# Five top-k steps moved to earlier slots, sparse scores in groups, and the first slabs' cuts on one engine, in a hybrid decoder block on one core

## The reference

```python
h = rmsnorm(x, norm_mix)
q_sb,k_sb,v_sb, q_sa,k_sa,v_sa, q_idx,k_idx,w_idx, g_sb,g_sa = split(h @ w_in)
# branch A, 8 heads: stick-breaking attention
z = q_sb @ k_sb.T / 8                               # q, k normed per head
attn = exp(log_sigmoid(z) + sum over later keys j<t of log_sigmoid(-z))   # strictly causal
o_sb = attn @ v_sb
# branch B, 8 heads, 2 key heads: sparse attention
score = sum over 8 index heads of w_idx * relu(q_idx @ k_idx.T / sqrt(32)) # causal
idx = top_k(score, 128)                             # per query
s = q_sa @ k_sa[idx].T / 8 - slope * distance ;  o_sa = softmax(s) @ v_sa[idx]
x = x + (sigmoid(g_sb) * (o_sb @ w_branch_sb) + sigmoid(g_sa) * (o_sa @ w_branch_sa)) @ w_out
x = x + relu(rmsnorm(x, norm_mlp) @ w_ff1)**2 @ w_ff2
```

## Time and profile before

| | |
|---|---|
| median of 3 runs | 729.56 us (729.49 to 729.64) |
| profiled execution | 729.32 us, its span 727.6 us |
| TensorE busy | 721.1 us (99% of the span) |
| VectorE, ScalarE, GpSimd busy | 523.4, 336.1, 242.7 us |
| HBM | 93 GB/s over the span |

### The profile page before, as it was taken

The page is one execution under the profiler, slowest core; times in us unless marked ns, Lnnn a source line. Parts: engine busy times, 40 slices in busy tenths (PEclk is TensorE's granted clock), DMA queues, the critical chain, the costliest instruction groups (busy, mean ns, idle before and its releaser), DMA issues.

```text
span 727.6 us, 9748 instructions
## 1 busy us (share of the span) xinstructions
PE 721.1 (99%) x3456; PEld 575.6 (79%) x3456; DVE 523.4 (72%) x757; ACT 336.1 (46%) x483; POOL 242.7 (33%) x197
## 2 busy tenths in 40 slices
PE   8999999999999999999999999999999999999998
PEld 5878788787776666788889988888888888888887
DVE  7355887899986865537746569695968778695972
ACT  6244753465567777722334353534344252535320
POOL 4005226011224663003301091815336180816610
DMA  9309231311111202133190225151331505131102
GB/s 327 145 15 264 84 117 58 116 59 59 59 59 36 78 11 52 59 116 115 45 331 5 78 92 175 59 173 58 118 112 54 177 0 182 49 115 58 58 16 101
DMA packets 44037, 70.62 MB, mean 97 GB/s; under 512 B 2657, under 2 KB 27489, under 8 KB 44002
## 3 DMA queue, kind: packets, MB, share of 16 engines
q1 hardware_dynamic: 44000, 70.16, 29.6%
q10 hardware_dynamic: 2, 0.00, 0.0%
HBM read 65.71 MB, written 2.10 MB: 93 GB/s over the span
## 4 chain that ended last, share of the span: by engine, by line
PE 92%; DVE 4%; ACT 1%; POOL 1%; issue 1%; DMA 0%; DVEq 0%; ACTq 0%; POOLq 0%
PE ps L1849 8%; PE ps L1848 8%; PE ps L1847 8%; PE ps L422 6%; PE ps L424 6%; PE ps L423 6%; PE ps L1875 6%; PE ps L1877 6%; PE ps L1876 6%; PE ps L415 6%; PE ps L417 5%; PE ps L416 5%; PE ps L1729 1%; PE ps L1665 1%; PE ps L1699 1%; PE ps L1761 1%
## 5 line engine op out<-in xcount | busy, mean ns | idle before, releaser
L1847 PE MATMUL ps<-b_hi,cut_hi 128*128 128x512 f32 (+1 forms) x280 | 104.0, 371 | 0.0
L1848 PE MATMUL ps<-b_lo,cut_hi 128*128 128x512 f32 (+1 forms) x280 | 103.8, 371 | 0.0
L1849 PE MATMUL ps<-b_hi,cut_lo 128*128 128x512 f32 (+1 forms) x280 | 103.8, 371 | 0.0
L422 PE MATMUL ps<-cut_hi,a_hi 128*128 128x512 f32 x216 | 86.5, 400 | 0.0
L424 PE MATMUL ps<-cut_hi,a_lo 128*128 128x512 f32 x216 | 84.5, 391 | 0.0
L423 PE MATMUL ps<-cut_lo,a_hi 128*128 128x512 f32 x216 | 84.3, 390 | 0.0
L917 ACT ACTIVATE qo_sb<-ps 128x512 f32<-128x512 f32 x32 | 19.1, 598 | 135.6 <-PE ps L1849 91.0
L636 POOL TENSOR_TENSOR a_lo<-qo_sb,a_hi 128x512 fp32r<-128x512 f32 x49 | 78.2, 1628 | 5.6 <-ACT a_hi L927 5.6
L406 DVE TENSOR_TENSOR cut_lo<-raw,cut_hi 128x2048 fp32r<-128x2048 f32 (+2 forms) x33 | 53.4, 1622 | 27.6 <-ACT cut_hi L398 27.6
L398 ACT ACTIVATE cut_hi<-raw 128x2048 fp32r<-128x2048 f32 (+2 forms) x33 | 48.5, 1468 | 31.1 <-PE ps L417 22.7
L1848 PEld LDWEIGHTS ps<-b_lo,cut_hi 128*128 128x128 f32 x280 | 52.8, 188 | 9.1
(11 more groups left out here) (210 smaller groups left out, 1678.3 us busy)
## 6 DMA issues: line engine op xcount, KB each, us to landing
raw<-in_w_ff_dram SPq DMA_DIRECT2D x32, 1024.0 KB, 5.6
raw<-in_w_in_dram SPq DMA_DIRECT2D x16, 1024.0 KB, 5.6
gates<-in_x_dram SPq DMA_DIRECT2D x8, 512.0 KB, 5.7
raw<-in_w_out_dram SPq DMA_DIRECT2D x4, 1024.0 KB, 5.1
raw<-in_w_in_dram SPq DMA_DIRECT2D x4, 512.0 KB, 7.1
raw<-in_w_branch_sb_dram SPq DMA_DIRECT2D x2, 1024.0 KB, 4.9
raw<-in_w_branch_sa_dram SPq DMA_DIRECT2D x4, 512.0 KB, 6.1
out_dram<-gates SPq DMA_DIRECT2D x7, 256.0 KB, 2.0
```

Of the source, the lines that this page charges most:

```text
L422: nc.tensor.matmul(dst, l_hi, w_hi, start=start, stop=False)
L1847: T.matmul(dst, w_hi[:, w], b_hi[:, k, a:b], start=(k == 0), stop=False)
L1848: T.matmul(dst, w_hi[:, w], b_lo[:, k, a:b], start=False, stop=False)
L1849: mm = T.matmul(dst, w_lo[:, w], b_hi[:, k, a:b], start=False, stop=(k == KD - 1))
```

## The change

Three edits.

1. The lower half of slab 1's low part goes from GpSimd (between its second and third row norm) to VectorE, between VectorE's two other cuts.
2. Top-k: two steps per token block in QSA where there was one, and five behind it where there were four; of the eight single steps in the sparse heads those at n = 8, 9 and 10 stay. The slots between keep their counts.
3. Scores: the pairs 0 to 3 (first token block) are computed together inside the last gate of the stick-breaking heads, pairs 4 and 5 together at pair 2 and pairs 6 and 7 together at pair 4; from pair 8 on it is one at a time as before. `score_bank` puts the pairs of a group side by side in the two banks that hold the scores, and `sa_logits` waits for the whole group. In the last stick-breaking pair the first head's sums come after one group of three gate matmuls in place of two.

```diff
--- before.py
+++ after.py
@@ -429,6 +429,12 @@
         def gate_bank(f):
             return 6 if f == 0 or f >= 8 and f % 2 else 7
 
+        def score_bank(n):
+
+            b, r = divmod(n // 2, GQ)
+            a = (r * P, r % 2 * 2 * P, 0, 0)[b]
+            return bank(n % 2, a, a + (b + 1) * P)
+
         def sa_head(n):
 
             r, g = divmod(n % 8, SAKV)
@@ -568,11 +574,6 @@
                                    ALU.pow).then_inc(row_ready, 1)
 
             for m in range(TB):
-                if m == 2:
-                    pool.wait_ge(half_hi, 2)
-                    pool.wait_ge(half_cut, 1)
-                    pool.tensor_tensor(cut_slot(1, cut_lo, 0, 2), raw[:, 1, 0:SLAB // 2],
-                                       cut_slot(1, cut_hi, 0, 2).bitcast(F32), ALU.subtract).then_inc(half_cut, 1)
                 rows_rsqrt(m)
 
             n_norm = 0
@@ -1070,6 +1071,7 @@
             norm_lo(1, a_hi, a_lo)
             norm_scale(1, x_tok[:, 1, :], x_tok[:, 1, :], mix_gain)
             dve_cut(0, 1, 2)
+            dve_half(1)
             dve_cut(1, 1, 2)
             for m in range(2, TB):
                 norm_lo(2 * m - 2, a_hi, a_lo)
@@ -1188,7 +1190,7 @@
                             V.tensor_copy(k_stack[:, :], k_in)
                             V.tensor_copy(q_stack[:, 4:8, :], q_in[:, 4:8, :]).then_inc(ix_ready, 1)
                         if g >= KSB:
-                            topk(1)
+                            topk(2 if g == QSA else 1)
                         head_scaled(4 * g + m)
                 else:
                     for m in range(TB):
@@ -1198,7 +1200,7 @@
                 if g in (KSB, QSA):
                     dve_cut(2 * g + 3)
                 if g in (KSB, QSA):
-                    topk(4)
+                    topk(5 if g == QSA else 4)
 
             def zset(h):
                 return ps[:, 3 * (h % 2) * S:3 * (h % 2) * S + ZW]
@@ -1229,12 +1231,12 @@
             def sa_logits(n):
 
                 w, j = (n // 8 + 1) * P, n % 4
-                dve.wait_ge(s_done, n + 1)
+                dve.wait_ge(s_done, 8 if n < 8 else n // 4 * 4 + 4 if n < 16 else n + 1)
                 dve.wait_ge(bias_done, n + 1)
                 dve.wait_ge(tri_done, 7 if n < 2 else 8)
                 if n >= 4:
                     dve.wait_ge(pt_done, n - 3)
-                V.tensor_tensor_reduce(out=sa_s[j][:, 0:w], in0=bank(n % 2, 0, w), in1=sa_bias[j][:, 0:w],
+                V.tensor_tensor_reduce(out=sa_s[j][:, 0:w], in0=score_bank(n), in1=sa_bias[j][:, 0:w],
                                        scale=-1.0, scalar=3.0e38, op0=ALU.add, op1=ALU.min,
                                        accum_out=snmax[:, j:j + 1]).then_inc(smax_done, 1)
 
@@ -1266,7 +1268,7 @@
                 V.tensor_scalar(sa_s[j][:, 0:w], sa_s[j][:, 0:w], rcp_l[:, j:j + 1], None, ALU.mult).then_inc(pn_done, 1)
                 if n < 32:
                     sa_logits(n)
-                topk(1 if n in (4, 7, 8, 9, 10, 11, 12, 15) else 0 if n < 20 else 60)
+                topk(1 if n in (8, 9, 10) else 0 if n < 20 else 60)
                 if n % 8 in (5, 6) and n < 32:
                     if n == 5:
                         dve.wait_ge(lo_done, SL_GATE + 5)
@@ -1720,14 +1722,15 @@
                 if k1 == KD:
                     mm.then_inc(gate_done, 1)
 
-            def sa_scores(pair):
-                b, r = divmod(pair, GQ)
-                if pair:
-                    pe.wait_ge(smax_done, 2 * pair)
-                for g in range(SAKV):
-                    p = slice(64 * g, 64 * g + 64)
-                    T.matmul(bank(g, 0, (b + 1) * P), qT_sa[p, r, b * P:(b + 1) * P],
-                             k_sa[p, 0:(b + 1) * P], start=True, stop=True).then_inc(s_done, 1)
+            def sa_scores(first, count=1):
+                if first:
+                    pe.wait_ge(smax_done, 2 * first)
+                for pair in range(first, first + count):
+                    b, r = divmod(pair, GQ)
+                    for g in range(SAKV):
+                        p = slice(64 * g, 64 * g + 64)
+                        T.matmul(score_bank(2 * pair + g), qT_sa[p, r, b * P:(b + 1) * P],
+                                 k_sa[p, 0:(b + 1) * P], start=True, stop=True).then_inc(s_done, 1)
 
             pe.wait_ge(const_cut, 2)
             pe.wait_ge(tr_out, 16)
@@ -1740,16 +1743,16 @@
                 gate(2 * c)
                 if c:
                     weighted_values(c - 1)
-                gate(2 * c + 1, 0, 2)
+                early = 1 if c == 3 else 2
+                gate(2 * c + 1, 0, early)
                 sum_later(2 * c)
-                gate(2 * c + 1, 2, 6)
+                gate(2 * c + 1, early, 6)
                 sum_later(2 * c + 1)
                 if c == 3:
                     pe.wait_ge(a_done, 7)
-                    sa_scores(0)
+                    sa_scores(0, 4)
                 gate(2 * c + 1, 6, 8)
             weighted_values(3)
-            sa_scores(1)
 
 
             def sa_turn(n):
@@ -1781,7 +1784,10 @@
                     gate(15, *((0, 2), (2, 3))[pair - 14])
                 sa_turn(2 * pair + 1)
                 if pair < 14:
-                    sa_scores(pair + 2)
+                    if pair in (2, 4):
+                        sa_scores(pair + 2, 2)
+                    elif pair >= 6:
+                        sa_scores(pair + 2)
                     gate(8 + pair // 2, 4 * (pair % 2) + 2, 4 * (pair % 2) + 4)
                 if pair and pair % 2 == 0:
                     sa_values(pair // 2 - 1)
```

## The result

| | before | after |
|---|---|---|
| median | 729.49 us (729.21 to 729.65, 20 runs) | 730.58 us (729.94 to 731.34, 20 runs) |
| profiled execution | 729.32, span 727.6 | 730.15, span 728.4 |
| ratio | | 1.0015 (95%: 1.0009 to 1.0021) |

The change costs 1.09 us, 0.15%: less than the 0.2% that was set as the limit of "same", and measurable all the same. The forecast was 730.2 and "same".

What follows compares the result with a forecast made beforehand. TensorE was taken as the bound, busy 721.1 of 727.6 us. The terms -0.73 + 1.1 + 1.5 - 1.8 - 1.0 + 1.5 = +0.6 gave 729.9 profiled, 730.2 median; range 728.1 to 731.6.

Steps and rivals of the forecast that it cites:

- First slabs: Slabs at the start: three equal VectorE cuts without GpSimd's piece end TensorE's wait at 16.47; gain 0.73, bounds 0 and 0.73.
- rival (d): First slabs gain nothing because GpSimd's norms stretch three cuts: 730.9; chance 0.49 together with the forecast.
- Moved steps: Sparse query norms and the slot behind them: five extra top-k steps fit into VectorE's idle time and cost nothing.
- Pair 0 and pair 2: Stick-breaking heads: wider top-k steps in unchanged slots delay VectorE's cuts, so TensorE loses 1.1 and another 1.5.
- Rival (c): Stick-breaking heads don't pay, since slack at the sums is larger than the rows say: 727.6; chance 0.15.
- the terms of the value projection: Wider steps in its slots: two grow 0.3 each, 0.35 lost in idleness, third 1.24 less 0.2; first softplus 1.15 later.
- 12.0 for 9.8, less 0.20: Pair 1's slot: eight 512-column steps take 12.0 where 9.8 was taken, less idle time; put at 2.1 later.
- Grouped scores: Sparse-head score pairs joined in groups pay for columns alone, the fixed part once per group: TensorE saves 1.8.
- Rival (a): Joined score pairs don't stream behind one another, 1.0 in all: 731.2; chance 0.20, shared with waits at upper bounds.
- Sparse heads: TensorE's two waits for scaled weights go, -1.0; new waits at n = 4, 5, 8, 9, 12, 13 cost 1.5.
- Rival (b): Sparse heads find no new wait because ScalarE's half cut starts early enough: 728.7; chance 0.16.

Runs made afterwards that it cites:

- edit 1 undone: The changed kernel with GpSimd again making the lower half of slab 1's low part: median 730.93 us, ratio to before 1.0011 to 1.0029.
- the slots kernel: Changed kernel with top-k slots 1, 1, 4 (value projection) and 7 (pair 1), sparse-head steps at n = 8, 12, 15, 16, 17: 727.34 us.
- edit 3 alone: The kernel before with only the grouped scores and the last pair's first sums three matmuls earlier: 729.06 us, ratio 0.9986 to 1.0004.
- edit 2 alone: The kernel before with only the changed top-k slots: 730.80 us, ratio 1.0010 to 1.0028.
- the half-cut kernel: The changed kernel with ScalarE's second half cut of the gate slabs one head earlier (n = 3, 11): 729.09 us, ratio 0.9986 to 1.0004.
- the early matmuls: The changed kernel with top-k slots and half cut repaired, plus two matmuls on zeros before all else: 725.92 us, ratio 0.9939 to 0.9966.

## Why the prediction was right, and where it was not

The mechanism was right place by place; one term, the gain in the first slabs, was mis-sized. The forecast was +0.6 and +1.09 was measured; this term makes 0.3 to 0.4 of the difference of 0.5.

- **First slabs**, -0.73 forecast: -0.35 (edit 1 undone) to -0.45 (alone) in the medians. The three cuts became equal and the wait went, as said. By the Trainium skill (GPSIMD Engine Reference, Specifications), GpSimd shares its SBUF interface with VectorE; the trace agrees, with 1.22 per cut when GpSimd's large piece is gone. What failed is the last step, that every later start moves up by the whole wait. It took the pace of TensorE in the one trace at hand (full from 10.06 on) as given. The best execution has the forecast start (16.39 against 16.45); where the pace changes later or the tokens land later, that is what is late next, and up to all of the gain is lost: in the four traces of the changed kernel line 423 starts at 16.92, 17.25, 16.62 and 17.40, against 17.41 before. Single executions gain nothing, as rival (d) had it, but not by its mechanism: no cut is stretched, all three take 1.22, and the medians do gain.
- **Moved steps**, 0 forecast: 0; the idle times shrank from 1.28 and 1.52 to 0.30 and 0.79.
- **Pair 0 and pair 2**, +1.1 and +1.5 forecast: +1.14 and +1.50. Shown by the slots kernel, in which both are given back. Rival (c), that the slack is larger, falls. Two small slips stand in the forecast's working: the terms of the value projection add up to 1.3 and not 1.15 (measured were 1.16: the first softplus starts at 144.71 in place of 144.04, while TensorE is 0.50 earlier), and 12.0 for 9.8, less 0.20, is 2.0 later and not 2.1.
- **Grouped scores**, -1.8 forecast: -1.79, worked out as a remainder from edit 3 alone; of the 1.0 for pairs 1 to 3, 1.00 is read directly. Rival (a), joined pairs paying singly, falls with the 1.09 us of four pairs. By the Trainium skill (TensorEngine Tiling (Array Packing), Key Properties) a change of mode, not of the tile, drains TensorE; the trace agrees that the fixed part is paid once per group, whatever it is.
- **Sparse heads**, -1.0 and +1.5 forecast: waits of 1.03 go, worth 1.29 with edit 2 alone, and new waits of 0.32, 0.20, 0.35, 0.31 and 0.33 come at n = 4, 5, 8, 12 and 13, 1.5. With the grouped scores the stretch was forecast at -1.3; from its first scores to n = 13 the matmuls gain 1.37. Rival (b), that ScalarE's cut starts early enough, falls; the half-cut kernel shows that moving this cut removes the waits at n = 4, 5 and 12 and half of that at n = 13; the slots kernel removes the one at n = 8.

Behind the first slabs the forecast was 1.1 + 1.5 - 1.8 - 1.0 + 1.5 = +1.3. The profiled executions show +1.21 to +1.32 behind line 422, and 0.11 more behind line 423, to which the forecast counts. The edits alone, -0.03, +1.40 and -0.39, add up to +0.98. The missing 0.2 to 0.3 lies in the sparse heads, where edit 2 alone gains 1.29 and edit 3 alone 0.42, and both together 1.37, 0.34 less than their sum. How the two edits hinder each other there is not shown.

## What to carry to other kernels

When work is taken by position from one ordered list, moving some of it earlier changes every slot behind: read what each later slot will hold, and what it will cost there, before counting the gain. A wait that is taken away in front of the bound engine is worth only the distance to what is late next, and at the start of a kernel that distance differs from one execution to the next, so one trace is too few for it. Gains on the bound engine can be lost at once to engines that ran just in time; here two small repairs, one step fewer in each of two slots and one cut a head earlier, turned +1.1 us into -3.5.

## What the runs showed of the hardware

TensorE's pace at the start was not expected. In ten of the fourteen traces its first 512-column matmuls on the slabs start 0.43 us apart, which is 512 columns at 1.2 GHz, and after some moment 0.23 apart, near 2.4 GHz; in the other four the change falls into the second interval already (0.29 to 0.37). That moment lies between about 9.3 and 12.3 us, and differs between executions of one and the same kernel (about 10.8, 10.3, 9.4 and 11.6 in the changed one). Before it, TensorE was idle until its first load landed (2.3 to 3.3 us; 1.3 with the early matmuls), then ran four single-row matmuls, one on zeros, eight transposes and the first matmuls, with at most 0.4 of idle time in a row. The granted clock in the profile's rows reads 1.00 throughout, so this is seen from the starts alone. What sets the moment stays open.

GpSimd's piece did not stretch the two cuts of VectorE beside it alike. Taken singly, the first cut of the kernel before (start 11.85) takes 1.22 although GpSimd's piece begins at 12.00, and the whole loss is in the second, which ends 1.09 us after GpSimd's end at 15.33 (timeline of VectorE from 13.2 on, where it stands unmerged):

```profile
12.99 3.43 DVE L406 TENSOR_TENSOR cut_lo<-raw,cut_hi 128x1024 fp32r<-128x1024 f32 x1
```

In the three other kernels with this piece the second cut takes 3.43, 3.43 and 3.39. Why the first is spared, no run here shows.
